# Where the rows of a gate come from: 32 matmuls in the first two expert passes, or a store and two broadcast loads

## The chip, the core and the metric

One NeuronCore of a Trainium2 chip runs the whole kernel. The metric is the device time in microseconds of one execution. TensorE (PE in the profile) multiplies matrices into eight PSUM banks, VectorE (DVE), ScalarE (ACT) and GpSimd (POOL) work element by element, SyncE (SP) does nothing but issue transfers, and 16 DMA engines carry them. ACT and POOL can issue transfers too.

## The reference, cut to what matters

One layer over 384 tokens of width 1024: 128 context tokens and 256 latent tokens. A modulation vector of six parts is computed from a conditioning vector, one vector for context tokens and one for latent tokens. After four token mixers comes a mixture of experts, and its output is scaled by the last of the six parts, `g2`, before it is added:

```
x = x + g1 * mix
h = _rmsnorm(x, p["norm2_g"]) * (1.0 + sc2) + sh2
x = x + g2 * _moe(h, p)
```

There are 64 experts; each token goes to eight. An expert has two matrices of 1024x256 (gate and up) and one of 256x1024 (down), so 3 MB of float32. After the last addition a final RMS norm is taken. `g2` differs between context and latent tokens but not between the tokens of one kind: tokens lie on partitions, so each of the two vectors is wanted as a row of 1024 repeated on all 128 partitions.

## The kernel before

The program has two parts. The *trunk* (projections, mixers, shared expert, router) runs to about 846 us of the span. Then `experts` (L2714) works on passes. A pass takes two experts of one slot `a_` (0 or 1): it gathers tokens (`xg`), multiplies by gate and up (job `H`), lets ACT and DVE form the hidden values, transposes them (`HT`), multiplies by down (`Y`) and scatters the result into PSUM banks 0 to 5 (`scatter`), where the sums of all tokens stay until the end. A round is two passes, slots 0 and 1. `body(0, "first")` is the first round, a hardware loop runs the others ("mid"; up to some count with four parts of a pass in 3+1, then in halves), and `body(n2, "last")` is one more pass.

Weights are double buffered by slot. SP issues them in `sync_part`: `refill` loads the four gate/up matrices of a slot (L3333, 1 MB each) once `H` of that slot is filled, and the two down matrices (L3337) once `Y` is filled. SP works its list in order. Ahead of the first refill it stores three tiles of token rows (L3347; the third waits for a GpSimd addition that itself waits for VectorE to have taken job `X 2`), then loads the final gain as a broadcast row (L3350), then waits for `X 2` and reads expert numbers out of SBUF.

The first round has extra jobs, since the assignment of experts to passes is still being planned: `X 0` to `X 4` are small matmuls of the plan (VectorE works between them), `G0` gathers, `S0` turns a selection, and `B 0` to `B 3` make the rows of the last gate. `gate_row` (L2874) is one `B` job: for each of four blocks of 128 channels two matmuls (a high and a low part) of a broadcast column of `mod_parts` with the identity, 8 matmuls into one PSUM bank, which ACT copies into `g2row` (L3022). All of these use banks 6 and 7, by the table `FIRST_BANKS`; a job waits until the job that had its bank before was read. `BETWEEN` says after which step `k` of `H` a job is put: `B 0` behind step 5 of the first `H`, `B 2` and `B 3` behind steps 4 and 6 of the second; `B 1` stands between the first `H` and `HT`. `mod_parts` is made by two VectorE operations (L2353, L2354) late in the trunk, and TensorE waits for them at L1181.

`g2row` is read only at the very end (L3257, L3260), when the expert sums are complete.

The first gate's rows go another way already: ACT stores `mod[:, 16:24]` to a DRAM tensor, one element per partition and channel block (L1681), and later loads it back as two broadcasts (L1701).

## Time and profile before

| | us |
|---|---|
| median of three runs | 1392.11 |
| lowest and highest of them | 1391.52, 1392.51 |
| span of the profiled execution | 1392.6 |
| PE busy | 1355.8 (97%) |
| DVE, ACT, POOL busy | 600.6, 390.8, 313.7 |
| granted TensorE clock | 9 or more tenths in 39 of 40 slices |
| DMA share by slice, from slice 25 of 40 | 9 tenths or more up to the last slice |

The span is the time from the first to the last instruction of one execution on the chip; the device times of the three other executions lie within 1.1 us of it. The profile gives for each engine how long it was busy; since matmuls are pipelined, a busy PE is not a PE at its peak. Times below are counted from the start of the span.

### The profile page before, as it was taken

Reading aid. Unit: us, or ns where it says so; the run is one execution under the profiler, and the core shown is the slowest. Engines: PE = TensorE matmul, PEld = TensorE weight load, DVE = VectorE, ACT = ScalarE, POOL = GpSimd, SP = SyncE. Lnnn points to the kernel's source line nnn. Section 1 sums busy time; section 2 is a strip of 40 time slices with the busy share of each in tenths; the row PEclk is TensorE's granted clock in tenths of the full one; section 3 lists DMA queues with packets and bytes.
Section 4 is the critical chain, followed back from the end, with each engine's and each line's share of the span. In section 5 each row is a group of like instructions: output and inputs, shape, how many; then the busy total and the mean of one; then the engine's idle time right before and its main releaser. Section 6 shows DMA issues by size and latency. Waiting matters only on the chain.

```text
span 1392.6 us, 20702 instructions
## 1 busy us (share of the span) xinstructions
PE 1355.8 (97%) x7716; PEld 950.3 (68%) x7716; DVE 600.6 (43%) x1347; ACT 390.8 (28%) x769; POOL 313.7 (23%) x248
## 2 busy tenths in 40 slices
PE   7999999999999999999999999999999999999996
PEld 2695898989988996788988875444445444444453
DVE  3467451885545486533322266333222332322224
ACT  3232221322544255233431141222112211221122
POOL 0431232243135553553333001101000000000001
PEclk9999999999999999999999999999999999999998
DMA  9640423133213336812144536999999999999992
GB/s 355 212 136 1 137 91 121 35 118 92 92 61 92 106 122 270 285 51 48 61 136 137 165 121 264 392 414 421 419 420 421 421 421 420 421 419 420 420 417 85
DMA packets 109744, 321.54 MB, mean 231 GB/s; under 512 B 12489, under 2 KB 72649, under 8 KB 81136
## 3 DMA queue, kind: packets, MB, share of 16 engines
q1 hardware_dynamic: 98416, 307.64, 57.6%
q0 software_dynamic: 2560, 8.81, 1.6%
q10 hardware_dynamic: 8704, 4.20, 1.1%
q8 instruction: 44, 0.72, 0.2%
q14 instruction: 20, 0.16, 0.0%
HBM read 320.08 MB, written 4.33 MB: 233 GB/s over the span
## 4 chain that ended last, share of the span: by engine, by line
PE 86%; DMA 9%; DVE 2%; ACT 1%; POOL 1%; issue 1%; SPq 0%; DVEq 0%; POOLq 0%
PE banks L650 21%; PE banks L617 20%; PE banks L2933 12%; DMA w<-in_exp_w 7%; PE banks L2980 7%; PE banks L2835 6%; PE banks L1057 3%; PE banks L2820 2%; PE banks L624 2%; PE banks L1201 1%; DMA ring<-in_ada_w 1%; PE banks L2828 1%; PE banks L769 1%; PE banks L889 1%; PE banks L701 1%; PE banks L1260 1%
## 5 line engine op out<-in xcount | busy, mean ns | idle before, releaser
L2933 PE MATMUL banks<-w,xg 128*64 128x512 f32 (+1 forms) x1312 | 235.8, 594 | 2.0 <-DMA w<-in_exp_w 1.9
L2933 PEld LDWEIGHTS banks<-w,xg 128*64 128x64 f32 (+1 forms) x1312 | 72.1, 126 | 150.9 <-issue 126.4
L650 PE MATMUL banks<-hT,ring 128*128 128x192 f32 x792 | 137.7, 327 | 0.2 <-DMA ring<-in_w_in 0.2
L3310 POOL DMA_INDIRECT fetched<-token_rows,row_of_place x32 | 32.1, 1004 | 443.2 <-DVE row_of_place L3111 433.1
L650 PEld LDWEIGHTS banks<-hT,ring 128*128 128x128 f32 x792 | 129.6, 190 | 2.1 <-DMA ring<-in_w_in 0.8
L2980 PE MATMUL banks<-w,hidT 128*64 128x512 f32 (+1 forms) x656 | 122.6, 600 | 0.3 <-DMA w<-in_exp_w 0.2
L2835 PE MATMUL banks<-y,selT 128*128 128x512 f32 x384 | 115.0, 415 | 0.0
L650 PE MATMUL banks<-x,ring 128*128 128x192 f32 x528 | 97.0, 327 | 0.9 <-ACT late L1377 0.9
L650 PE MATMUL banks<-x,combos 128*128 128x192 f32 x528 | 96.6, 326 | 0.0
L3122 DVE SCALAR_TENSOR_TENSOR hid<-banks,gslot,sil 128x256 f32<-128x256 f32 x33 | 16.0, 484 | 178.3 <-ACT sil L3015 177.7
L2835 PEld LDWEIGHTS banks<-y,selT 128*128 128x128 f32 x384 | 66.3, 189 | 35.1 <-issue 26.2
L650 PEld LDWEIGHTS banks<-x,ring 128*128 128x128 f32 x528 | 86.9, 190 | 1.4 <-ACT late L1377 1.2
L650 PEld LDWEIGHTS banks<-x,combos 128*128 128x128 f32 x528 | 87.6, 190 | 0.0
L617 PE MATMUL banks<-yT,ring 128*128 128x384 f32 x256 | 86.3, 487 | 0.9 <-ACT yT L1285 0.9
L617 PE MATMUL banks<-ring,hT 128*128 128x256 f32 x384 | 84.0, 379 | 0.0
L1285 ACT ACTIVATE arena<-banks 128x512 f32<-128x512 f32 (+2 forms) x91 | 49.7, 575 | 114.7 <-PE banks L617 57.1
L617 PEld LDWEIGHTS banks<-ring,hT 128*128 128x128 f32 x384 | 72.6, 190 | 10.2 <-issue 0.6
L2980 PEld LDWEIGHTS banks<-w,hidT 128*64 128x64 f32 (+1 forms) x656 | 32.1, 125 | 66.5 <-issue 46.8
L2480 POOL TENSOR_TENSOR ring<-ring,combos 128x512 f32<-128x512 f32 x33 | 44.9, 1360 | 131.4 <-PE banks L650 131.1
L3131 DVE TENSOR_TENSOR y<-banks,y 128x512 fp32r<-128x512 f32 x66 | 45.6, 691 | 62.5 <-ACT y L3034 62.5
L3015 ACT ACTIVATE sil<-banks 128x256 f32<-128x256 f32 x33 | 12.7, 384 | 201.4 <-PE banks L2933 201.4
L617 PEld LDWEIGHTS banks<-yT,ring 128*128 128x128 f32 x256 | 47.5, 190 | 29.3 <-issue 1.1
(482 smaller groups left out, 2033.4 us busy)
## 6 DMA issues: line engine op xcount, KB each, us to landing
w<-in_exp_w SPq DMA_DIRECT2D x198, 1024.0 KB, 13.9
ring<-in_w_in SPq DMA_DIRECT2D x46, 1024.0 KB, 5.5
ring<-in_ada_w SPq DMA_DIRECT2D x24, 1024.0 KB, 6.9
ring<-in_w_branch SPq DMA_DIRECT2D x8, 1024.0 KB, 6.6
ring<-in_w_out SPq DMA_DIRECT2D x4, 1024.0 KB, 6.6
arena<-in_sh_w SPq DMA_DIRECT2D x3, 1024.0 KB, 8.4
x<-in_x_sample SPq DMA_DIRECT2D x4, 512.0 KB, 8.3
token_rows<-whole_rows SPq DMA_DIRECT2D x3, 384.0 KB, 20.1
```

What stands on the lines that cost most here:

```text
L617: last = mm(out, lhsT=lhsT, rhs=rhs, start=i == 0, stop=i == len(pairs) - 1)
L624: last = nc.tensor.transpose(ps[0:n, i * P:(i + 1) * P], src, ident[:, :])
L650: last = mm(out, lhsT=w[:, k, :], rhs=tokens[:, k, :], start=start and k == 0, stop=k == KD // 2 - 1, skip_group_check=not start)
L1057: last = mm(ps[:, h * P:(h + 1) * P], lhsT=lhsT, rhs=rhs, start=True, stop=True)
L1285: banks.free(on(out, banks.at(act, key) if "src" not in kw else kw.pop("src"), func, **kw), key)
L2480: s_combos.on(g.tensor_tensor(a11, a12, combos[:, 1], ALU.subtract))
L2820: last = mm(out[:, i * 256:i * 256 + 256], lhsT=h2[part][:, t, k * P:(k + 1) * P], rhs=sel[:, t, :, :], start=n == 0, stop=n == 2 * NT - 1)
L2835: ins = mm(psum[:, t * 2 + h, :], lhsT=selT[:, a_, t * P:(t + 1) * P], rhs=y[:, part, h * W:(h + 1) * W], start=False, stop=False)
L2933: ins = mm(ps[lo:hi, :], lhsT=xg[:, k, a_ * P + lo:a_ * P + hi], rhs=w13[:, a_, u, :, k, :], start=k == 0, stop=k == KD - 1)
L2980: ins = mm(ps[lo:hi, :], lhsT=hidT[:, f, lo:hi], rhs=w2[:, a_, u, f, h * W:(h + 1) * W], start=f == 0, stop=f == 1)
L3131: ins = tt(y[:, LO, hh], ps, y[:, HI, hh].bitcast(F32), ALU.subtract)
L3310: nc.gpsimd.indirect_dma_start(fetched[:, a_, :], None, rows[:, :], bass.IndirectOffsetOnAxis(ap=row_of_place[:, 2 * a_:2 * a_ + 1], axis= ...
```

## The change

The rows of the last gate are no longer made by matmuls. ACT stores `mod[:, 40:48]` to a second DRAM tensor beside the first gate's, and SP loads it back as two broadcasts of 512 KB, behind the final gain and ahead of the first refill. The matmuls, the four jobs, the ACT copies, the two VectorE operations and the wait on them go; `X` jobs that had their bank after a `B` job now have it after another. VectorE waits for the two loads ahead of its first use of `g2row`.

```diff
-        mod_parts = sb("mod_parts", P, 2, KD, 2, dt=F32R)
+        sb("unused_parts", P, 4 * KD)
...
-            pe.wait_ge(s_row_parts.sem, 1)
...
                         act.dma_start(gate_rows[cnd].rearrange("(k p) -> p k", p=P), mod[:, 16:24, cnd],
                                       allow_slow_non_contiguous=True).then_inc(s_stored_gates.sem, 16)
+                        act.dma_start(last_gate_rows[cnd].rearrange("(k p) -> p k", p=P), mod[:, 40:48, cnd],
+                                      allow_slow_non_contiguous=True).then_inc(s_stored_last.sem, 16)
...
-            lane.link(v.tensor_copy(mod_parts[:, 0], mod[:, 40:48, :]))
-            s_row_parts.on(tt(mod_parts[:, 1], mod[:, 40:48, :], mod_parts[:, 0].bitcast(F32), ALU.subtract))
...
-                   ("X", 0, 1): 6, ("S0", 1, 0): 6, ("B", 0, 0): 6, ("X", 0, 2): 6, ("H", 0, 0): 7, ("B", 0, 1): 6, ("HT", 0, 0): 7,
-                   ("X", 0, 3): 6, ("Y", 0, 0): 7, ("X", 0, 4): 6, ("Y", 0, 1): 7, ("S", 0, 0): 7, ("S", 1, 0): 7, ("B", 0, 2): 7,
-                   ("B", 0, 3): 7}
+                   ("X", 0, 1): 6, ("S0", 1, 0): 6, ("X", 0, 2): 6, ("H", 0, 0): 7, ("HT", 0, 0): 7,
+                   ("X", 0, 3): 6, ("Y", 0, 0): 7, ("X", 0, 4): 6, ("Y", 0, 1): 7, ("S", 0, 0): 7, ("S", 1, 0): 7}
...
-               (0, 5): ("B", 0, 0), (0, 6): ("X", 0, 2), (1, 1): TURNS[0], (1, 2): TURNS[1], (1, 4): ("B", 0, 2), (1, 6): ("B", 0, 3)}
+               (0, 6): ("X", 0, 2), (1, 1): TURNS[0], (1, 2): TURNS[1]}
...
-                else:
-                    add_job(("B", 0, 1))
...
+        dve.wait_ge(s_g2, 32)
         for t in range(NT):
             dve.wait_ge(s_summed, t + 1)
             tt(gated[:, t, 0:W], psum[:, t * 2, :], g2row[:, min(t, 1), 0:W], ALU.mult).then_inc(s_gated, 1)
...
         sp.dma_start(fg_row[:, :], a["final_g"].rearrange("(a n) -> a n", a=1).to_broadcast([P, D])).then_inc(s_fg, 16)
+        sp.wait_ge(s_filled, 1)
+        sp.wait_ge(s_stored_last.sem, 32)
+        for cnd in range(2):
+            sp.dma_start(g2row[:, cnd, :], last_gate_rows[cnd].rearrange("(a n) -> a n", a=1).to_broadcast([P, D])).then_inc(s_g2, 16)
         sp.wait_ge(s_read["dve"], read(0, "dve", ("X", 0, 2), "first"))
```

## Rows read from the trace of the kernel before

**Rows 1.** Chain that ended last, in time order: start us, length us, what.

```profile
928.71 6.87 PE banks L2933 x64
...
1174.89 6.87 PE banks L2933 x32
...
1206.13 20.34 DMA w<-in_exp_w
...
1324.51 21.48 DMA w<-in_exp_w
```

**Rows 2.** Windows: stretch, length, busy us of five engines, PE clock, DMA share, GB/s.

```profile
875.00:1346.00 471.00, 468.40 (x2722) 223.28 (x2721) 139.86 (x387) 93.84 (x184) 31.12 (x31) 1.00 1.01 420
```

**Rows 3.** Tile of the expert weights: three slot-0 gate/up refills, issue and landing.

```profile
L3333 SPq DMA_DIRECT2D w<-in_exp_w x4: 333/354/1018, 919.4 to 920.9; - x4
DMA to landing us min/median/max: 8.5/11.5/14.7
...
L3333 SPq DMA_DIRECT2D w<-in_exp_w x4: 333/356/381, 1042.5 to 1043.9; - x4
DMA to landing us min/median/max: 10.6/13.6/17.1
...
L3333 SPq DMA_DIRECT2D w<-in_exp_w x4: 333/356/380, 1196.3 to 1197.8; - x4
DMA to landing us min/median/max: 12.5/15.9/21.6
```

**Rows 4.** Timeline, 865 to 884: start us, us, engine, line, operation, idle before.

```profile
865.81 0.34 PE L2868 MATMUL banks<-plan,late 64*1 64x24 f32 x4 [0.31 <-DVE plan L3194]
...
869.65 0.31 PEld L2949 LDWEIGHTS banks<-ident,hid 128*128 128x128 f32 x2 [0.21 <-DVE hid L3122]
...
870.27 0.17 PEld L2868 LDWEIGHTS banks<-plan,late 64*1 64x1 f32 x4 [0.30 <-ACT g2row L3022]
...
882.77 1.11 PE L2881 MATMUL banks<-ident_r,mod_parts 128*128 128x128 f32 x8
883.81 1.94 PE L2933 MATMUL banks<-w,xg 128*64 128x512 f32 x8
```

**Rows 5.** Timeline of GpSimd and of SP's queue, 868 to 905.

```profile
868.57 1.81 POOL L3299 TENSOR_TENSOR whole_rows<-h_high,h_low 128x768 f32<-128x768 f32 x1 [27.23 <-DVE quarter_gates L3202]
...
870.82 0.38 SPq L3350 DMA_DIRECT2D final_gain<-in_final_g  x1
...
873.11 2.02 SPq L3333 DMA_DIRECT2D w<-in_exp_w  x4
...
905.05 2.04 SPq L3333 DMA_DIRECT2D w<-in_exp_w  x4
```

**Rows 6.** Windows (as rows 2) where transfers ran below full rate.

```profile
719.90:723.90 4.00, 4.00 (x19) 3.07 (x19) 1.11 (x2) 0.70 (x2) 2.08 (x3) 1.00 0.84 276
722.00:723.00 1.00, 1.00 (x8) 1.00 (x7) 0.56 (x1) 0.00 (x0) 0.19 (x1) 1.00 0.94 377
871.10:875.00 3.90, 3.90 (x22) 2.12 (x21) 1.29 (x5) 0.60 (x1) 0.59 (x1) 1.00 0.98 269
905.00:908.00 3.00, 3.00 (x16) 2.54 (x16) 0.81 (x3) 1.13 (x3) 0.00 (x0) 1.00 0.98 388
937.00:939.00 2.00, 2.00 (x13) 1.70 (x12) 0.33 (x2) 0.83 (x2) 0.00 (x0) 1.00 0.97 360
```

**Rows 7.** Timeline round the first gate's store, 625 to 683.

```profile
625.94 1.01 ACTq L1681 DMA_DIRECT2D gate_rows<-mod  x2
629.86 0.33 ACT L1387 ACTIVATE late<-banks 128x192 f32<-128x192 f32 x1 [3.60 <-PE banks L650]
...
675.95 7.07 PE L617 MATMUL banks<-ring,hT 128*128 128x256 f32 x32
```

**Rows 8.** Tile of the ring: one slab's load and its landing.

```profile
L2599 SPq DMA_DIRECT2D ring<-in_w_in x1: 582/582/582, 621.1 to 621.1; - x1
...
DMA to landing us min/median/max: 14.6/14.6/14.6
```

More of the change, by code:

```diff
@@ L223, in trunk @@
         ident_r = sb("ident_r", P, P, dt=F32R)
-        mod_parts = sb("mod_parts", P, 2, KD, 2, dt=F32R)
-        gate_rows = nc.dram_tensor("gate_rows", (2, D), F32, kind="Internal").ap()
+        sb("unused_parts", P, 4 * KD)
+        gate_rows, last_gate_rows = (nc.dram_tensor(name, (2, D), F32, kind="Internal").ap()
+                                     for name in ("gate_rows", "last_gate_rows"))
         branches = ctx.enter_context(ExitStack())
@@ L470, in trunk @@
         s_madd = sig("branch_terms_added")
-        s_row_parts = sig("gate_row_parts_ready")
+        s_stored_last = sig("last_gate_rows_stored")
         s_stored_gates, s_g1 = sig("first_gate_rows_stored"), sig("first_gate_rows_landed")
@@ L603, in trunk @@
         s_w13 = [ctx.enter_context(nc.semaphore(f"gate_up_{a_}_landed")) for a_ in range(2)]
-        expert_work = experts(ctx, nc, a, o, psum, x, h2, mod_parts, ident_r, ident, ss, sq, sums, places, gates, iota, tiles, s_w13,
-                              s_rowsT.sem, s_out)
+        expert_work = experts(ctx, nc, a, o, psum, x, h2, last_gate_rows, ident_r, ident, ss, sq, sums, places, gates, iota, tiles, s_w13,
+                              s_rowsT.sem, s_out, s_stored_last)
         block = ctx.enter_context(nc.Block())
@@ L2711, in expert_tiles, with experts @@
     ])
-def experts(ctx, nc, a, o, psum, x, h2, mod_parts, ident_r, ident, ss, sq, sums, places, gates, iota, tiles, s_w13, s_rowsT, s_out):
+def experts(ctx, nc, a, o, psum, x, h2, last_gate_rows, ident_r, ident, ss, sq, sums, places, gates, iota, tiles, s_w13, s_rowsT, s_out, s_stored_last):
     def sem(name):
@@ L2753, in experts @@
     s_gated, s_added = sem("sums_gated"), sem("first_halves_added")
-    s_fg = sem("final_gain_landed")
+    s_fg, s_g2 = sem("final_gain_landed"), sem("last_gate_rows_landed")
     s_x = sem("second_halves_added")
@@ L2778, in readers @@
         kind, _, i = job
-        return {"H": ("act", "dve"), "HT": ("act",), "S": ("act",), "S0": ("act",), "Y": ("act", "dve"), "X": ("dve",), "B": ("act",),
+        return {"H": ("act", "dve"), "HT": ("act",), "S": ("act",), "S0": ("act",), "Y": ("act", "dve"), "X": ("dve",),
                 "G": (("act",), ("dve",))[i % 2], "G0": (("act",), ("dve",))[i % 2]}[kind]
@@ L2873, in plan_step @@
             return mm(out[:, NX:2 * NX], lhsT=rowsE[0:NE, 1, t * P:(t + 1) * P], rhs=one_hot, start=True, stop=True)
-        def gate_row(i, out):
-            cnd, h = divmod(i, 2)
-            for j in range(4):
-                for part in (HI, LO):
-                    c = mod_parts[:, part, h * 4 + j, cnd:cnd + 1]
-                    ins = mm(out[:, j * P:(j + 1) * P], lhsT=c.to_broadcast([P, P]), rhs=ident_r[:, :],
-                             start=part == HI, stop=part == LO)
-            return ins
         def body(q, kind, quarters):
@@ L2905, in add_job @@
                     close_bank(plan_step(i, open_bank(job)))
-                elif what == "B":
-                    close_bank(gate_row(i, open_bank(job)))
                 elif what == "G0":
@@ L3019, in take @@
                 ins = on(xg[:, 2 * i:2 * i + 2, :].rearrange("p k n -> p (k n)"), ps, ACT.Copy)
-            elif what == "B":
-                cnd, h = divmod(i, 2)
-                ins = on(g2row[:, cnd, h * W:(h + 1) * W], ps, ACT.Copy)
             elif what == "S0":
```

## The prediction

> **What bounds the kernel now.** The page comes first: PE is busy 97% of the span, which suggests that matmuls removed are time gained. It is an average over two different parts. From slice 25 on the line of DMA shares stands at 9 tenths or more, so the second view is the windows of that part: from 875 to 1346 us the engines moved 420 GB/s with a share of 1.01 and never rested [rows 2]. Two resources are near their limits at once, and the question is which one ends last.
>
> The chain of waits answers it round by round. Up to about 1206 us it runs through PE alone; rounds begin at 928.71 and, eight rounds later, at 1174.89, so PE needs (1174.89 - 928.71) / 8 = 30.8 us for one [rows 1]. Then the chain goes through transfers of expert weights of some 20 us each, the last of them issued at 1324.51 and waited for until 1346.0 [rows 1]. What follows 1346 is PE's fixed tail.
>
> How it comes to that is in the landings [rows 3]. The last of the four gate/up loads of slot 0 lands at 920.9 + 14.7 = 935.6, four rounds later at 1043.9 + 17.1 = 1061.0, five later at 1197.8 + 21.6 = 1219.4, and four later at 1346.0 [rows 1]. That is 31.35, 31.7 and 31.65 us a round, against PE's 30.8. The transfers are the slower stream from the start. They begin with a lead (a landing 14.7 us after its issue, where PE first has to wait at 21.6), lose 0.5 to 0.9 us of it a round, and at 1219 it is gone. So the end is set by one thing: when the stream of expert weights starts, and how much it must carry. A start x us later makes the kernel x us longer, and PE has 21.6 - 14.7 = 6.9 us of slack in the early rounds, to be used up by whatever PE saves there.
>
> **Part by part.**
>
> *The matmuls.* Each of the four jobs takes 883.81 - 882.77 = 1.04 us of PE [rows 4]: 4.2 us in all. On PE's own path the first one gives nothing: the plan job after it waits for VectorE anyway until 865.81 [rows 4], and with the bank job gone PE would only wait there longer. The second stood in the time in which `HT` waits for the hidden values, until 869.65 [rows 4]; it gives at most the 0.30 us by which the following plan job waited for ACT's copy of its bank [rows 4]. The last two give 2 x 1.04. PE is then 0.3 + 2.1 = 2.4 us earlier at the end of the first round. This is time that the slack of 6.9 us takes up: PE comes to wait for transfers some rounds sooner. On the path that ends last I count it as 0; its bounds are 0 and -2.4 us, the latter if the stream followed PE. The ACT copies and two small vector operations are beside PE's work: 0.
>
> *When the stream starts.* SP's first refill is issued at 873.11 [rows 5]. Ahead of it are VectorE's reading of `X 2`, GpSimd's addition at 868.57 of 1.81 us, the third store, the load of the final gain at 870.82, and 1.9 us in which SP reads the expert numbers [rows 5]. `X 2` starts when the plan is ready, at 865.8 as before, so nothing in this row moves forward. SP gets two more issues of 0.38 us: the refill is issued 0.8 us later. The two added waits are for things long past (the first bank filled in the first round, and a store of the trunk), so they hold up nothing that is queued behind them on SP, the refills.
>
> *What the stream carries.* The two broadcasts write 2 x 0.524 = 1.05 MB, and they are ahead of the refill in the same queue. At the stream's 420 GB/s that is 2.5 us [rows 2]. The nearest rows are the first gate's own two broadcasts: from 719.9 on they ran at 276 GB/s, 1.05 / 0.276 = 3.8 us; the first half of it is slow, while the window 722 to 723 has 377 GB/s, at which both would take 2.8 us [rows 6]. I take 2.8, because the new pair follows a broadcast that is already flowing (the final gain) as the second of that pair did, and keep 2.5 and 3.8 as ends. Now the shift. Between 871.1 and 875 the engines moved 269 GB/s x 3.9 us = 1.05 MB [rows 6], of which the third store and the final gain are 0.39 + 0.52 = 0.92; the remaining 0.13 MB are experts, worth 0.3 us at full rate. So the stream started as if at 875 - 0.3 = 874.7, and some 0.3 us earlier the gain was through. The new start is 874.4 + 2.8 = 877.2: 2.5 us later. Ends: 2.2 and 3.5. The 0.8 us of issue lie within it, since the queue is busy with the broadcasts meanwhile.
>
> *What comes back.* In the rounds where the lead in the queue was thinnest the rate dipped: 388 GB/s for 3 us from 905, just when SP issued a refill at 905.05, and 360 for 2 us from 937 [rows 5, 6]. Short of 420 that is 0.10 and 0.12 MB, 0.5 us together. With the stream later and PE's issues earlier, the queue is no longer near dry there. Up to 0.5 us may come back, or nothing if the engine that lands last was not the one that rested; I take 0.3.
>
> *The store.* Two issues more on ACT's queue, 1.0 us. ACT idled 3.60 us before its next operation at 629.86 [rows 7], so this is hidden; without that cover it would be 1.0 us at most. The transfers are 2048 elements of four bytes. Beside the ones that exist, a slab load issued at 621.1 took 14.6 us to land [rows 8], and twice as many elements may at most double that: 621.1 + 29.2 = 650.3. The slab belongs to the projection that PE starts at 675.95 [rows 7]: 25 us of cover, cost 0. The other slab of the time is issued ahead of it in the same queue and so landed earlier; if it too were held, GpSimd's work on it would be late, which I bound at +1 us, the length of the two added issues. The Trainium skill ("DMA: Bandwidth & Descriptors", Rules for kernel authors) says that a last dimension that isn't contiguous becomes one descriptor per element and is to be rearranged. [...]
>
> *The end.* VectorE's new wait ahead of `g2row` is for loads that land at about 878, 500 us before it: 0.
>
> Sum: 0 (matmuls) + 2.5 (stream later) - 0.3 (dips) + 0 (store) = +2.2 us. Against the profiled execution that is a span of 1392.6 + 2.2 = 1394.8; the median of the runs is 0.5 lower, 1392.1, so 1394.3 us.
>
> **Rivals.**
>
> *A. PE's time counts.* If the stream were paced by PE in the first rounds (the dips at 905 and 937 speak for it a little), the refills would come 2.4 us sooner. Against it: the rate is 420 GB/s nearly everywhere, and the landings come farther and farther apart from PE's round. 1392.1 - 2.4 = 1389.7; all four jobs at full price, 1387.9.
>
> *B. The loads are hidden.* A load asked for before the third store would have the engines to itself; SP, though, is held by that store until GpSimd's addition ends at 868.57 + 1.81 = 870.4 [rows 5], and these loads come behind it. For B it would need that broadcasts and weights overlap without sharing a rate: then only the 0.8 us of issue stays, less 0.3: 1392.6. The Trainium skill ("DMA: Bandwidth & Descriptors", Rules for kernel authors) advises to issue a DMA early and wait on its semaphore late, so that its setup overlaps with work; by it this change costs nothing, B's time. What the rule leaves out is that rows 2 show no free share of the engines.
>
> *C. A deeper queue is a slower queue.* Landings are 31.35 us apart in the first four rounds, 31.65 once the queue is deep [rows 3]. If depth itself is what costs (engines falling out of step, gathers behind more weights), then the new kernel, whose lead is gone from about the third round instead of the tenth, pays the 0.3 us difference in four or more rounds, +1.3 us, and no dip comes back: 1392.1 + 2.5 + 1.3 = 1395.9. It decides as soon as PE waits for weights before about 1100 us. Against it: both stretches show the same 420 GB/s.
>
> **How the numbers follow.** My forecast 0.50, with its own range 1393.3 to 1395.4; A 0.13; B 0.17; C, or the broadcasts at their slow end, 0.20. The time is that of the first, 1394.3. The range of 8 in 10 takes in the others in part: 1390.4 to 1396.6. A change of under 0.2% (2.8 us) is about what can't be told from none: below 1389.3 lies only the far half of A, 0.07; above 1394.9 lie C and a quarter of the forecast, 0.33; the rest, 0.60, is within.
>
> **What would show it.** Right: the refill issued near 873.9; the window 871 to 878 full of broadcasts; `X 2` on PE still at 865.8; slot 1's first refill issued some 2.4 us earlier than before; PE's first wait for expert weights well before 1206; the last such wait ending near 1348.2 instead of 1346.0, with the same 1392.6 - 1346.0 = 46.6 us behind it. Wrong: first refill's stream beginning before 876 (B), the last wait ending before 1346 (A), landings more than 31.6 us apart in the first rounds (C), or PE late anywhere before 860 (the store).

## The result: 1406.98 us, 1.0% slower

| | before | after |
|---|---|---|
| median, same chip | 1392.11 us (5 runs, 1391.52 to 1395.13) | 1406.98 us (5 runs, 1404.59 to 1409.39) |
| span of the profiled execution | 1392.6 us | 1407.2 us |
| ratio, 95% interval | | 1.010, 1.0088 to 1.0112 |

The forecast was 1394.3 us with a range up to 1396.6. The change is slower by 14.9 us in the medians and by 14.6 us in the two profiled spans, and the loss is in three places, two of which (the store and the removed matmuls) the prediction had costed at nothing. One execution of all runs below, of the kernel with the turned rows, had a mean TensorE clock of 0.946 and took 1426.65 us; it is left out.

**The page after.** TensorE is busy 0.9 us longer, although 32 matmuls are gone. ACT's queue (q10) has 10,784 packets in place of 8,704, and they take 2.1% of the DMA engines' time in place of 1.1%: of the 2,080 packets more, 2,048 are the new store's elements of four bytes, 8 KB together.

```profile
PE 1356.7 (96%) x7684; PEld 947.1 (67%) x7684; DVE 599.6 (43%) x1345; ACT 388.0 (28%) x765; POOL 313.8 (22%) x248
q10 hardware_dynamic: 10784, 4.21, 2.1%
```

**The end of the loop.** First the chain of waits after, the answer to [rows 1] (start us, length us, what). It goes through the expert weights from 1157 us on instead of from 1206, and the last landing is at 1338.62 + 21.71 = 1360.3 where it was 1346.0: 14.3 us late. What follows it is 46.9 us against 46.6. So the whole loss is there when the loop ends.

```profile
1157.19 20.01 DMA w<-in_exp_w
...
1338.62 21.71 DMA w<-in_exp_w
```

Next the timelines of two engines after, first TensorE's with two of its waits, then SP's queue from 868 to 920 us; the answer to [rows 4, 5]. The final gain is issued at 878.37 instead of 870.82, so 7.55 us of the 14.3 are there before any expert weight is reloaded. The refill follows 2.99 us behind it (before: 2.29), the down matrices are issued at 888.33, and by 917.62 the list is 12.57 us behind the 905.05 of [rows 5].

```profile
872.92 0.34 PE L2867 MATMUL banks<-plan,late 64*1 64x24 f32 x4 [1.50 <-DVE plan L3176]
...
903.09 1.09 PE L2827 MATMUL banks<-ident,fetched 128*128 128x128 f32 x8 [2.06 <-DMA fetched<-token_rows,row_of_place]
...
878.37 0.38 SPq L3333 DMA_DIRECT2D final_gain<-in_final_g  x1
878.85 0.92 SPq L3337 DMA_DIRECT2D g2row<-last_gate_rows  x2
881.36 2.35 SPq L3316 DMA_DIRECT2D w<-in_exp_w  x4
888.33 0.81 SPq L3320 DMA_DIRECT2D w<-in_exp_w  x2
...
917.62 2.12 SPq L3316 DMA_DIRECT2D w<-in_exp_w  x4
```

**The trunk: 7.55 us between these two traces, 10.3 from the store on.** The change does nothing before the first gate's store, and that store is issued at 625.94 before [rows 7] and at 623.19 after. So the execution traced after was 2.75 us ahead when the change began to act. That is a difference between two executions and no gain: the two windows below, first before and then after, show one place where they differ: the granted clock is 0.86 in the trace before and 1.00 in the one after. The columns are stretch, length, busy us with counts for PE, PEld, DVE, ACT, POOL, PE clock, DMA share, GB/s. From the store to the final gain it is 870.82 - 625.94 = 244.9 us before and 878.37 - 623.19 = 255.2 us after, 10.3 us more. The ledger of the 14.3 us is -2.75 + 10.3 in the trunk and 6.75 in the expert part.

```profile
388.00:400.00 12.00, 11.60 (x84) 11.16 (x83) 5.96 (x22) 9.65 (x21) 0.00 (x0) 0.86 0.53 175
388.00:400.00 12.00, 11.60 (x97) 11.11 (x97) 7.28 (x24) 11.23 (x29) 1.14 (x1) 1.00 0.53 176
```

Where the 10.3 us go: windows after, 630 to 650 us. While the DMA engines are busy and move almost nothing (share 2.01, 5 GB/s), TensorE works 1.89 of 5 us and then 0 of 5, and its granted clock goes to half (0.69 and 0.62 are means over windows in which it changed).

```profile
630.00:635.00 5.00, 5.00 (x31) 3.94 (x31) 0.24 (x1) 3.07 (x6) 3.50 (x3) 1.00 1.59 1
635.00:640.00 5.00, 1.89 (x17) 1.69 (x15) 0.56 (x1) 0.00 (x0) 1.00 (x1) 1.00 2.01 5
640.00:645.00 5.00, 0.00 (x0) 0.00 (x0) 0.00 (x0) 0.41 (x1) 0.00 (x0) 0.69 0.83 25
645.00:650.00 5.00, 4.71 (x18) 3.91 (x19) 2.32 (x6) 1.33 (x3) 1.27 (x1) 0.62 0.77 167
```

The timeline of the same stretch shows who stood still (start us, us, engine, line, operation, idle before). ACT issues the four stores from 623.19 on, one of them in 2.85 us; that is the cover of 3.6 us of [rows 7], now 4.25, and harmless. Then at 636.9 TensorE's block of matmuls L1058 ends in the records, ACT should copy its bank, and no engine does anything until 644.59: ACT rests 10.52 us, VectorE 9.52, TensorE 8.40, GpSimd 11.39.

```profile
623.19 0.37 ACTq L1681 DMA_DIRECT2D gate_rows<-mod  x1
623.60 0.60 ACTq L1683 DMA_DIRECT2D last_gate_rows<-mod  x1
624.23 2.85 ACTq L1681 DMA_DIRECT2D gate_rows<-mod  x1
...
634.94 1.95 PE L1058 MATMUL banks<-arena 128*128 128x128 f32 x16
...
644.59 0.60 ACT L1285 ACTIVATE arena<-banks 128x512 f32<-128x512 f32 x1 [10.52 <-remote]
645.22 0.69 DVE L2345 TENSOR_TENSOR arena<-arena 128x512 f32<-128x512 f32 x1 [9.52 <-ACT arena L1285]
...
645.29 1.09 PE L625 MATMUL banks<-ident,arena 128*128 128x128 f32 x4 [8.40 <-issue]
...
648.16 1.27 POOL L2574 TENSOR_TENSOR arena<-arena,levels 128x512 f32<-128x512 f32 x1 [11.39 <-PE banks L1058]
```

What ACT waited for is called "remote" in this view, but the trace's records of semaphores, which none of the views prints, have it: it is TensorE's own count of filled banks. It rises at 644.57 and 644.66, which is 8.6 and 7.8 us after the recorded ends (635.99 and 636.88) of the two matmuls that raise it; before, it rises 0.02 us after each of the same two. GpSimd's count rose meanwhile, at 636.78, 0.01 us after its addition ended. So TensorE's signals were late, and not all signals; the other engines stood behind them. No load of program code is in the trace between 626 and 649 us, so the rest is no wait for one.

**The other 6.75 us (14.3 - 7.55), in the expert part.** Windows after. From 878.6 to 886 the engines moved 276 GB/s x 7.4 us = 2.04 MB, of which third store, gain and broadcasts are 1.97; the 0.07 MB of experts are 0.2 us at full rate, so their stream starts as if at 885.8, where it was 874.7: 11.1 us late, or 3.55 more than the trunk. Between 917 and 920 the queue runs dry at 191 GB/s, (419 - 191) x 3 / 419 = 1.6 us.

That leaves 1.6 us. Most of it is no late stream but a wider spread inside a group of four loads. The last two lines are the landings of the last four gate/up loads, before and after: the first lands at 1323.1 + 11.0 = 1334.1 and 1337.2 + 9.4 = 1346.6, 12.5 us late, the last 14.3 us late. The stream as a whole is thus some 12.7 us late (7.55 + 3.55 + 1.6), and TensorE waits for the last load of the four. What spreads them isn't shown.

```profile
878.60:886.00 7.40, 7.40 (x28) 3.91 (x28) 1.82 (x7) 0.98 (x2) 0.64 (x1) 0.62 0.95 276
872.00:882.00 10.00, 7.92 (x28) 4.30 (x30) 4.49 (x21) 0.77 (x2) 3.12 (x2) 0.60 0.31 94
910.00:917.00 7.00, 7.00 (x66) 1.98 (x64) 2.06 (x5) 0.60 (x1) 0.00 (x0) 1.00 1.01 410
917.00:920.00 3.00, 3.00 (x18) 2.32 (x15) 0.48 (x1) 1.11 (x3) 0.00 (x0) 1.00 0.64 191
920.00:1360.00 440.00, 436.86 (x2528) 206.97 (x2526) 130.03 (x360) 86.70 (x171) 28.93 (x29) 1.00 1.01 419
...
L3333 SPq DMA_DIRECT2D w<-in_exp_w x4: 333/357/381, 1323.1 to 1324.5; - x4
DMA to landing us min/median/max: 11.0/14.7/21.5
...
L3316 SPq DMA_DIRECT2D w<-in_exp_w x4: 333/356/381, 1337.2 to 1338.6; - x4
DMA to landing us min/median/max: 9.4/13.5/21.7
```

In this execution the granted clock was 0.60 in the window from 872 to 882, behind the 1.50 us in which TensorE waited for VectorE's plan with the first gate-row job gone ([rows 4]: 0.31). 0.50 is the 1.2 GHz level, 1.00 the 2.4 GHz level.

### The profile page after: what moved, and what is told of

Same layout as the page of the kernel before. It is cut to its first block, busy times and chain, and to the rows that moved or that the text cites. A ratio compares the mean times of both kernels' runs of the same rounds, so it can differ in the third digit from the quotient of the medians.

```text
span 1407.2 us, 20637 instructions
## 1 busy us (share of the span) xinstructions
PE 1356.7 (96%) x7684; PEld 947.1 (67%) x7684; DVE 599.6 (43%) x1345; ACT 388.0 (28%) x765; POOL 313.8 (22%) x248
## 3 DMA queue, kind: packets, MB, share of 16 engines
q10 hardware_dynamic: 10784, 4.21, 2.1%
q0 software_dynamic: 2560, 8.81, 1.6%
## 4 chain that ended last, share of the span: by engine, by line
PE 81%; DMA 13%; DVE 2%; issue 2%; ACT 1%; POOL 1%; SPq 0%; POOLq 0%; DVEq 0%
PE banks L651 21%; PE banks L618 20%; PE banks L2920 11%; DMA w<-in_exp_w 10%; PE banks L2965 7%; PE banks L2834 5%; PE banks L1058 3%; PE banks L2819 2%; PE banks L625 2%; PE banks L1201 1%; DMA ring<-in_ada_w 1%; PE banks L2827 1%; PE banks L890 1%; PE banks L770 1%; PE banks L702 1%
## 5 line engine op out<-in xcount | busy, mean ns | idle before, releaser
L2965 PE MATMUL banks<-w,hidT 128*64 128x512 f32 (+1 forms) x656 | 125.7, 610 | 0.5 <-DMA w<-in_exp_w 0.3
L3000 ACT ACTIVATE sil<-banks 128x256 f32<-128x256 f32 x33 | 12.7, 384 | 209.7 <-PE banks L2920 209.7
```

What stands on the lines that cost most here:

```text
L2965: ins = mm(ps[lo:hi, :], lhsT=hidT[:, f, lo:hi], rhs=w2[:, a_, u, f, h * W:(h + 1) * W], start=f == 0, stop=f == 1)
```

## Experiments: the change taken apart

Each time below is the median of 4 to 12 executions, with the lowest and the highest. "Before" is the kernel before on the same chip and at the same time: 1392.62 us for the first four, 1393.07 for the next four, then 1392.99, 1391.94 and 1392.44.

**The change without its store.** The broadcasts read the first gate's rows, so the output is not the reference's.

```diff
-        expert_work = experts(ctx, nc, a, o, psum, x, h2, last_gate_rows, ident_r, ident, ss, sq, sums, places, gates, iota, tiles, s_w13,
-                              s_rowsT.sem, s_out, s_stored_last)
+        expert_work = experts(ctx, nc, a, o, psum, x, h2, gate_rows, ident_r, ident, ss, sq, sums, places, gates, iota, tiles, s_w13,
+                              s_rowsT.sem, s_out, s_stored_gates)
...
-                        act.dma_start(last_gate_rows[cnd].rearrange("(k p) -> p k", p=P), mod[:, 40:48, cnd],
-                                      allow_slow_non_contiguous=True).then_inc(s_stored_last.sem, 16)
```

> The changed kernel without the added store of elements; the two broadcasts read the first gate's rows instead, so the last gate's values are not the reference's. Theory S (the store's 2048 four-byte packets hold up the trunk: in the changed kernel every engine rests for 8.4 us at 637 to 645): the rest goes, the trunk ends 7.4 us earlier, about 1399.6 us. Rival (the rest comes from something else that was changed, such as the removed wait or the two vector operations): still about 1407.

Measured: 1398.14 us (1396.0 to 1399.16), ratio 1.0038 (1.0024 to 1.0052). The store carries some two thirds of the loss.

**The removal alone.** No store and no loads; `g2row` is set to ones by GpSimd, so the last gate is left out.

```diff
-        for cnd in range(2):
-            sp.dma_start(g2row[:, cnd, :], last_gate_rows[cnd].rearrange("(a n) -> a n", a=1).to_broadcast([P, D])).then_inc(s_g2, 16)
...
+        nc.gpsimd.memset(g2row[:, :, :], 1.0).then_inc(s_g2, 1)
```

> The matmuls, their jobs and copies are removed and nothing is put in their place: no store, no loads; the rows of the last gate are set to 1 by GpSimd, so that gate is left out of the result. Theory C (the hole left by the first job makes TensorE rest, its clock falls to half for 10 us, the later passes are late and the transfer queue runs dry): slower than before by 3 to 5 us, 1395 to 1397, with half clock near 867 to 877 and a dip in transfers near 910. Rival L (only the loads cost anything): 1392 or a little below.

Measured: 1394.39 us (1392.46 to 1400.04), ratio 1.0015 (1.0004 to 1.0026). Taking 32 matmuls out of a kernel whose TensorE is busy 97% of the time makes it slower, not faster, though by less than the 3 to 5 us that I had expected. In its windows TensorE runs at half clock behind the hole, and by 902 to 912 the weights are below full rate:

```profile
864.00:874.00 10.00, 8.84 (x26) 3.38 (x24) 3.30 (x14) 0.77 (x2) 4.86 (x3) 0.51 0.56 179
...
902.00:912.00 10.00, 10.00 (x80) 4.84 (x76) 3.69 (x12) 2.94 (x6) 2.00 (x2) 1.00 0.97 375
```

**The two broadcasts alone**, in the kernel before: they load the first gate's rows into `g2row`, and the `B` jobs stay, but ACT copies their banks (192 columns) into a scratch tile.

```diff
-                ins = on(g2row[:, cnd, h * W:(h + 1) * W], ps, ACT.Copy)
+                ins = on(tiles["scratch"][:, :], ps[:, 0:192], ACT.Copy)
...
+            sp.dma_start(g2row[:, cnd, :], gate_rows[cnd].rearrange("(a n) -> a n", a=1).to_broadcast([P, D])).then_inc(s_g2, 16)
```

> The kernel before with only the two broadcast loads added (of the first gate's rows); the matmul jobs stay and their copies go to a scratch, 192 columns each, so the last gate's values are not the reference's. If the stream's later start passes through to the end: +3.5 us, 1395.6 (broadcasts at some 280 GB/s). If broadcasts run at the stream's rate: +2.2, 1394.3. Theory C says no half clock here. Rival (hidden): 1392.5.

Measured: 1396.18 us (1394.61 to 1398.13), ratio 1.0022 (1.0013 to 1.0031). In the chain of this kernel (as above) TensorE waits for weights from 1082 us on. The last landing is at 1327.70 + 21.46 = 1349.2 instead of 1346.0, with the final gain issued at 870.56 instead of 870.82: 3.5 us for the pair, as expected. Behind the chain stand windows of this kernel. By 878 the engines had moved 259 GB/s x 3.8 + 300 x 3.4 us = 2.00 MB, of which 1.97 are third store, gain and broadcasts, so the weights start as if at 877.9, 3.2 us later than before. The last two are the places of the dips of [rows 6], and the dips are gone (before: 388 and 360 GB/s).

```profile
1082.63 20.41 DMA w<-in_exp_w
...
1327.70 21.46 DMA w<-in_exp_w
...
870.80:874.60 3.80, 3.80 (x22) 2.01 (x20) 1.33 (x5) 0.60 (x1) 0.63 (x1) 1.00 0.88 259
874.60:878.00 3.40, 3.40 (x18) 1.06 (x16) 2.73 (x9) 0.60 (x1) 0.00 (x0) 1.00 0.74 300
905.00:908.00 3.00, 3.00 (x19) 2.58 (x17) 0.81 (x4) 0.83 (x2) 0.00 (x0) 1.00 1.02 423
937.00:939.00 2.00, 2.00 (x16) 1.65 (x19) 0.55 (x4) 0.83 (x2) 0.00 (x0) 1.00 1.03 430
```

**The store alone**, added to the kernel before; nothing reads it.

```diff
+                        act.dma_start(last_gate_rows[cnd].rearrange("(k p) -> p k", p=P), mod[:, 40:48, cnd],
+                                      allow_slow_non_contiguous=True).then_inc(s_stored_last.sem, 16)
```

> The kernel before with only the second store of elements added beside the first gate's. Theory S: +7.4 us, 1399.5, with the same rest of all engines after 637. Rival (the store is hidden and the rest needs the other edits): 1392.

Measured: 1402.3 us (1400.28 to 1404.58), ratio 1.0069 (1.0055 to 1.0083). The same rest stands in its trace, TensorE idle 8.61 us until 645.68, and from the first gate's store to the final gain it is 255.4 us, 10.5 more than before. The parts add up, each as its median over 1392.62: store 9.7, loads 3.6, removal 1.8, together 15.0 (unrounded), against 14.9 for the whole. Loads and removal together are 5.3, and the run without the store had 5.5.

## Experiments: what it is about the store

**Half of it**: the kernel before with the second store for one condition only.

```diff
+                        if cnd: act.dma_start(last_gate_rows[cnd].rearrange("(k p) -> p k", p=P), mod[:, 40:48, cnd],
+                                      allow_slow_non_contiguous=True).then_inc(s_stored_last.sem, 16)
```

> The kernel before with the second store for one condition only: 1,024 elements more than before, where the full second store has 2,048 and cost 9.6 us (1402.3 against 1392.6). Theory 1, the loss grows with the number of single-element packets in flight: in proportion it gives +4.8 us, 1397.4 us, and the rest of all engines near 637 to 644 us is shorter. Theory 2, there is a number of packets below which nothing happens (the 2,048 of before show no rest): 1392.5 to 1394 us. Theory 3, the number of issued stores counts and not the packets: near three quarters or more of the full loss, 1399 us or above.

Measured: 1393.88 us (1391.99 to 1395.49), ratio 1.0001 (0.9992 to 1.0010). Not in proportion: 1,024 packets more cost at most 1.4 us, 2,048 cost 9.7. The trace still has a small rest of the same kind: TensorE 2.26 us until 646.93, and again the semaphore records show TensorE's own counts rising 3.0 and 1.8 us after the ends of their matmuls. From the first gate's store to the final gain this execution takes 247.4 us, 2.5 more than before; it is the slowest of the eleven (1395.49 us). So a hold is first seen with the 3,072 elements of the three stores, and little of it reaches the median. Packets of ACT's queue between 620 and 660 us take 3.8% of the engines' time before (2,080 packets), 9.3% here (3,120) and 37.7% after (4,160): 11.7 ns, 19 ns and 58 ns recorded for one packet (share x 16 engines x 40 us / packets). Recorded packets overlap where the share is above 1, as in the windows above, so the last is no time that an engine gave to one packet alone.

```profile
646.45 0.33 ACT L1372 ACTIVATE gate<-banks 128x192 f32<-128x192 f32 x1 [3.75 <-remote]
...
646.93 1.54 PE L652 MATMUL banks<-x,combos 128*128 128x192 f32 x8 [2.26 <-ACT gate L1372]
```

**The same numbers in 64-byte pieces.**

```diff
+                    act.dma_start(packed_rows, mod[:, 40:48, :].rearrange("p k c -> p (k c)")).then_inc(s_stored_last.sem, 16)
```

> The kernel before with one added store of the same 2,048 numbers at the same place, but as 64 contiguous bytes of each partition (nothing reads it). If the single-element packets are what holds the engines, this costs 0 to +1 us (1392.4 to 1393.6 us) and ACT's issue is short. If any transfer that ScalarE adds there costs the time, it comes out near the 1402.3 us of the store by elements.

Measured: 1393.37 us (1391.5 to 1395.45), ratio 1.0000 (0.9991 to 1.0009). The cost is the packets, not the transfer or its issue. That one issue takes 3.28 us, longer than the 2.85 us above (I had expected a short one), so a long issue is not the loss here either. The Trainium skill ("DMA: Bandwidth & Descriptors", Rules for kernel authors) says that a last dimension that isn't contiguous becomes one descriptor per element and should be rearranged; this pair of runs prices the rule here, 9.7 us against nothing.

**The store moved to 713 us**, the end of ACT's part of the delta mixer, in the changed kernel.

```diff
             fill("end")
+            for cnd in range(2):
+                act.dma_start(last_gate_rows[cnd].rearrange("(k p) -> p k", p=P), mod[:, 40:48, cnd],
+                              allow_slow_non_contiguous=True).then_inc(s_stored_last.sem, 16)
             act.wait_ge(s_stored_gates.sem, 16 * 2)
```

> The changed kernel with its added store issued at the end of the delta stage (near 715 us) in place of at 623 us. Theory: the loss of the store is that of its place, inside the levels of the inverse, where every engine hands over to the next each microsecond; at 715 us ScalarE has few hand-overs ahead, so the time falls to that of the kernel without the store, 1398 us (1397 to 1400). Rival: the packets hold the engines wherever they are issued, so 1405 to 1409 us, with a rest of all engines behind 715 us in the trace.

Measured: 1407.14 us (1405.54 to 1412.72), ratio 1.0106 (1.0089 to 1.0124). My theory fell: nothing was won. But the rival's picture is not what the trace shows either. Its timeline has a plain reason: ACT's next four issues stand behind the element packets in the same queue and take 4.45 and 9.34 us (before: 0.82 and 1.25), so ACT rests 14.31 us ahead of its next operation (before: 1.55), and TensorE waits 8.81 us for it.

```profile
713.53 1.00 ACTq L1700 DMA_DIRECT2D last_gate_rows<-mod  x2
714.57 4.45 ACTq L1704 DMA_DIRECT2D arena<-gate_rows  x2
719.07 9.34 ACTq L1708 DMA_DIRECT2D out_new_gdn<-arena  x2
728.43 1.28 ACT L1394 ACT_TABLE_LOAD   x1 [14.31 <-issue]
...
731.03 2.90 PE L651 MATMUL banks<-x,combos 128*128 128x192 f32 x8 [8.81 <-ACT gate L1370]
```

**The store moved to 655 us**, away from both neighbours.

```diff
+                    if (r, l) == (2, 4):
+                        for cnd in range(2):
+                            act.dma_start(last_gate_rows[cnd].rearrange("(k p) -> p k", p=P), mod[:, 40:48, cnd],
+                                          allow_slow_non_contiguous=True).then_inc(s_stored_last.sem, 16)
                     s_gmix.on(on(in_blocks(gmix, m), both_ways(GXT + r * 2 * W, m), ACT.Copy))
```

> The changed kernel with its added store issued at the fourth level of the last inverse, near 660 us: some 36 us behind the store of the first gate's rows and 55 us ahead of ScalarE's next transfers. Theory 1, what costs is how many single-element packets are in flight together, or what ScalarE issues behind them: each store alone drains in some 15 us, so the engines never rest for 8 us and the time is that of the change without its store, 1398 us, ratio 1.003 to 1.005. Theory 2, it is the total of 4,096 packets, or a second such store anywhere: 1405 to 1407 us, ratio 1.009 to 1.011.

Measured: 1402.08 us (1401.14 to 1405.34), ratio 1.0075 (1.0062 to 1.0088): between the two theories, 0.0037 or 5.2 us above the run without the store, 3.5 and 4.3 us below the same kernel with the store early and late (1.0100 and 1.0106). Nobody stands still now, and ACT's issues take 1.0 us. The victim is a third one: SP's ring load of 661.62 takes 10.5 us to land (before: 5.4), and TensorE waits for it 3.93 us and then runs at 0.64 clock for 4.8 us.

```profile
672.21 2.75 PE L651 MATMUL banks<-hT,ring 128*128 128x192 f32 x8 [3.93 <-DMA ring<-in_w_in]
...
672.20:677.00 4.80, 4.79 (x19) 4.79 (x20) 0.00 (x0) 0.54 (x2) 4.47 (x4) 0.64 0.32 120
```

So one store has three ways to cost, by its place: TensorE's signals come late and all engines stand behind them, the issuer's next transfer stands behind it, another queue's load lands late. Each way is read from one or two traces. The Trainium skill ("DMA: Bandwidth & Descriptors", Queues, rings and completion order) has it that each DMA engine takes turns between the queues it has work for, packet by packet; the late ring load agrees with it (10.5 us instead of 5.4).

## Experiments: the loads and the hole

**The broadcasts behind the last refill**, in the kernel without the store.

```diff
             refill(q, 0, bass.ds(2 * q, 1), "mid")
+
...
+        for cnd in range(2):
+            sp.dma_start(g2row[:, cnd, :], gate_rows[cnd].rearrange("(a n) -> a n", a=1).to_broadcast([P, D])).then_inc(s_g2, 16)
```

> The changed kernel without its added store, its two broadcast loads (of the first gate's rows) moved from ahead of the first refill to behind the last one. Theory 1, the pair costs 3.6 us because it stands ahead of the weight stream: moved, the time is that of the removal alone, 1394.4 us, ratio 1.001 to 1.002, and in the trace the pair lands by 1360 us, before its first use near 1377 us. Rival: the loads cost the same wherever they stand (they share the engines with the last landings, or the end waits for them): ratio 1.0035 to 1.004 as before the move.

Measured: 1393.63 us (1392.5 to 1400.2), ratio 1.0011 (1.0000 to 1.0022); ahead of the refill it was 1.0038, and the removal alone had 1.0015. The pair is issued at 1346.6, lands later than expected, by 1347.0 + 20.7 = 1367.7, and is first used at 1377.0. The 3.6 us are the price of the place, and all of it comes back.

```profile
L3238 DVE TENSOR_TENSOR w<-banks,g2row x3: 680/680/682, 1377.0 to 1378.2; 128x512 f32<-128x512 f32 x3
...
L3353 SPq DMA_DIRECT2D g2row<-gate_rows x2: 335/380/424, 1346.6 to 1347.0; - x2
...
DMA to landing us min/median/max: 14.4/17.6/20.7
```

**The final gain behind the last refill too**, in the kernel before, with the plan's wait and the reading of the expert numbers put ahead of the third store: the same lever pulled the other way.

```diff
             e = [sp.value_load(expert_of[0:1, u, at], min_val=0, max_val=NE - 1) for u in range(2)]
+            if kind == "first":
+                whole(NT - 1)
...
             refill(q, 0, bass.ds(2 * q, 1), "mid")
+
...
+        sp.dma_start(fg_row[:, :], a["final_g"].rearrange("(a n) -> a n", a=1).to_broadcast([P, D])).then_inc(s_fg, 16)
```

> The kernel before with only SyncE's list changed: the wait for the plan and the reading of the experts' numbers stand ahead of the third rows store, and the broadcast load of the final gain stands behind the last refill in place of ahead of the first. Theory 1, all that stands ahead of the weight stream is paid in full: the first refill is issued 2 to 3 us earlier and the stream is one load of the final gain (some 1.5 us) shorter, so 3 to 4 us faster, 1389 to 1390 us, ratio 0.997 to 0.998. Rival: TensorE, not the stream, sets the end over much of the loop, so the stream's start gives back 1 us or nothing: ratio 0.999 to 1.000.

Measured: 1393.2 us (1391.81 to 1395.4), ratio 0.9999 (0.9990 to 1.0008). A miss. The first refill is issued at 871.00 instead of 873.11, but the next are issued at 888.05 and 905.12, where they were at 887.98 and 905.05, because they wait for TensorE to empty a slot. The queue runs out of work meanwhile and the 2.1 us are lost again. In the windows of this kernel:

```profile
890.00:895.00 5.00, 4.65 (x32) 3.55 (x32) 1.32 (x3) 1.28 (x3) 0.00 (x0) 1.00 0.95 364
905.00:910.00 5.00, 5.00 (x32) 3.51 (x36) 1.98 (x8) 1.29 (x4) 1.00 (x1) 1.00 0.92 316
```

The same windows before had 414 and 398 GB/s. So the stream's start is a bound in one direction only here: later (the pair) costs in full, 2.1 us earlier gives nothing.

**Fillers in the holes**: the removal alone, with eight matmuls of the identity by itself in the place of the first removed job, then also in that of the second. A third has the first filler on the kernel with the late store.

```diff
+                    for j in range(8):
+                        ins = mm(ps[:, j // 2 * P:(j // 2 + 1) * P], lhsT=ident_r[:, :], rhs=ident_r[:, :], start=j % 2 == 0, stop=j % 2 == 1)
```

> The run with the removal alone (no store, no loads, the gate rows set to one), with eight matmuls of an identity by itself in the place of the first removed gate-row job. Theory 1, the removal made the kernel slower (ratio 1.0015) because of the hole that it left before TensorE's plan job, behind which the granted clock fell to 0.50 for 10 us: filled, the mean clock is back at 0.996 to 0.997 and the time at or below that of before, ratio 0.998 to 1.000. Theory 2, the loss is in the other three removed jobs, or in a changed order of the banks: ratio 1.001 to 1.003 as without the filler.

> The run with the removal alone, with fillers of eight matmuls of an identity by itself in the places of the first two removed gate-row jobs (ahead of the plan job, and between the first pass's first product and its turn). Theory 1, the loss by the removal (ratio 1.0015, executions with a mean clock of 0.991 to 0.995) is the holes: with both filled every execution has a mean clock of 0.995 or more as the kernels with all gate-row jobs have, and the time is 1391 to 1393 us, ratio 0.9985 to 1.000. Theory 2, the holes of the second pass or other things are it: some executions stay at 0.994 or below and the ratio at 1.0005 to 1.0015.

> As the run with the late store, and in the place of the removed first gate-row job TensorE runs eight matmuls of an identity by itself into a scratch bank (a filler, of no use to the result). Theory: the hole of the removed job lets TensorE's granted clock fall to 0.50 in some executions and puts the first refills late; filled, the clock stays at 1.00 and the time is 1 to 2.5 us below that of the late store alone, near 1396.5 us. Rival: the hole costs nothing by itself and the filler adds its own 0.5 us: same time or 0.5 us above.

Measured: one filler 1393.86 us (1390.81 to 1398.89), ratio 1.0009 (0.9997 to 1.0022); two 1392.67 us (1391.3 to 1395.82), 1.0005 (0.9997 to 1.0014); with the late store 1407.2 us, 1.0098 (1.0084 to 1.0113), no different from the same kernel unfilled. By the times alone neither theory is settled: the intervals overlap that of the bare removal. The clocks say more. Executions with a mean granted clock of 0.994 or less: 10 of 11 with the bare removal, 6 of 12 with one filler, 3 of 12 with two, and 0 of the 113 executions of the kernel before that were taken beside the experiments. So holes do cost clock, and filling them brings it back in part; I had expected all of it. Within one kernel the clock and the time go together: with one filler the six executions at 0.993 or 0.994 took 1394.29 to 1398.89 us and the six at 0.996 or 0.997 took 1390.81 to 1393.43. It need not be the removal's whole price, though: the run without the store has the same matmuls removed and mean clocks of 0.995 to 0.996, and the parts still add up to its time. Where the rest is, the profiled execution with two fillers shows. With 2.1 us less work in the second pass TensorE comes early to the fetched rows (`fetch` is issued at 881.50, before: 881.52), and waits:

```profile
892.01 1.10 PE L2826 MATMUL banks<-ident,fetched 128*128 128x128 f32 x8 [2.03 <-DMA fetched<-token_rows,row_of_place]
...
892.00:896.00 4.00, 3.65 (x16) 2.11 (x18) 1.97 (x7) 0.60 (x1) 0.00 (x0) 0.62 1.00 416
```

The last two removed jobs are turned into a wait of 2.03 us and a second fall of the clock.

**The change mended**: store at 655 us, both fillers, broadcasts last.

> The whole change, mended in three places: the added store near 660 us, fillers in the places of the first two removed jobs, and the two broadcast loads behind the last refill. If the costs of the store, of the stream's late start and of the holes were all there was, nothing is left of the 14.4 us: 1391 to 1394 us, ratio 0.999 to 1.001, and no gain either, since the 16 matmuls that stay away are not on the path of the weight stream. If a cost remains that the theory does not know: above 1395 us.

Measured: 1398.21 us (1397.14 to 1401.52), ratio 1.0049 (1.0036 to 1.0061). Above my range. The theory left out that the store still costs at this place: 5.2 us there and 0.7 of the removal with two fillers make 5.9, against 6.3 for the whole.

**Without an added element store.** The first gate's stays. SyncE's list is in the order of the run with the final gain last. One gate-row job is left, of two matmuls that turn the 16 columns into 16 rows of 512 bytes; these are stored as they are and broadcast back behind the last refill.

```diff
+            for part in (HI, LO):
+                ins = mm(out[0:2 * KD, 0:P], lhsT=mod_parts[:, part].rearrange("p c k -> p (c k)"), rhs=ident_r[:, :],
+                         start=part == HI, stop=part == LO)
...
+        sp.dma_start(last_gate_rows.rearrange("c (k p) -> (c k) p", p=P), tiles["turned"][:, :]).then_inc(s_rows_out, 16)
```

> The order of SyncE's list as in the run with the final gain last, and the change made another way: of the four gate-row jobs (32 matmuls) one is left, of two matmuls that turn the last gate's 16 columns into 16 rows of 512 bytes; these are stored contiguously after the first refill, and the two broadcast loads stand behind the last refill. Theory: neither the held engines nor the stream's late start are there, so at least as fast as the run with the final gain last, 1388 to 1390 us, ratio 0.996 to 0.998. Rival: the hole of the removed matmuls (only two of eight stay in the first job) lowers the clock again and takes 1 to 2 us back: 1390 to 1392 us.

Measured: 1393.32 us (1390.12 to 1396.08), ratio 0.9996 (0.9983 to 1.0008), clocks 0.993 to 0.997. The 1388 to 1390 us of the theory did not come. The same with both holes filled:

> The run with the turned rows (ratio 0.9996, mean clocks of 0.993 to 0.997 and one outlier), with the first gate-row job filled up to eight matmuls and the second one's place filled by eight matmuls of an identity by itself. Theory, the holes are what scatters the clock: all executions at 0.995 or above, no outlier, and a ratio of 0.999 to 1.000, 1391 to 1393 us; nothing is gained over the kernel before, since the sixteen matmuls left out are beside the weight stream. Rival: the scatter stays as it was, so it comes from the second pass's removed jobs or from the loads at the end: clocks down to 0.993 again and a ratio of 0.9995 to 1.001.

Measured: 1391.53 us (1390.06 to 1396.06), ratio 0.9998 (0.9988 to 1.0008), as expected, but two of twelve clocks at 0.994. These two are the only forms of the change that are not slower, and neither is faster than the kernel before by anything that can be measured.

## Why the prediction was wrong, by its own steps

- **What bounds the kernel**: right as far as it went. The loop's end moved by what the stream lost, and the tail stayed (46.9 against 46.6 us). "A start x us later makes the kernel x us longer" held (3.5 to 3.6 us for the broadcasts). Its other direction, that an earlier start would gain, was never needed for the sum and is false (ratio 0.9999).
- **The matmuls, 0 (bounds 0 and -2.4)**: wrong in sign. The step said "with the bank job gone PE would only wait there longer". It waited 1.50 us instead of 0.31, as said, but a wait was not neutral: the granted clock fell to half behind it in the traces of the change and of the removal alone (mean clock 0.994 or less in 10 of the latter's 11 executions), and in the trace with two fillers the saved time of the second pass ended in a wait for fetched rows. Measured +1.8 us (ratio 1.0004 to 1.0026); a bound below 0 only was the mistake. How much of it the clock is stays open.
- **When the stream starts, +2.5 (ends 2.2 and 3.5)**: right mechanism, size off. The refill came 2.99 us behind the gain instead of 2.29, so the 0.8 us of issue were right; with the loads alone the weights started 3.2 us later, 3.5 with the final gain's own 0.26 us, and the pair cost 3.5 us at the loop's end, 3.6 in the medians. I had picked the rate of the second half of the older pair's transfer; the mean rate of that whole pair, 3.8 us [rows 6], was the nearer row.
- **What comes back, -0.3**: the mechanism came with the loads alone, where the dips were gone (423 and 430 GB/s), but the loop's end gained nothing by it: 3.5 us late at the start, 3.5 at the end. In the whole change the queue ran dry at 917 us instead, since the third refill was issued 12.57 us late, 5.0 more than the trunk, behind TensorE's half clock and its wait for fetched rows.
- **The store, 0 (up to +1)**: the failed step, 9.7 of the 14.9 us. It asked only when the slab beside it would land. That slab, now issued at 618.4, landed in 12.2 us, and the next one, issued at 629.8, in 22.8 instead of 9.9; no engine waited for either, so that part held. But twice the packets made TensorE's signals 8 us late and the engines rest 8.4 us and more, and no row of before showed such a thing at half the dose. The forecast's own sign for it, TensorE late before 860, is the one that came. The bound "+1, the length of the two added issues" bounded a different mechanism.
- **The end, 0**: right; the loads land 500 us before their use.
- **Rivals**: A and B are out. C's conditions came (TensorE waits for weights before 1100 us in the run with the loads alone), but not its extra cost of 1.3 us: landings of that run are 31.5 us apart in the first four rounds and the shift at the end is 3.5 us, the pair itself. What was missing is a rival in which the store holds up the trunk, at a price of its own: 9.7 us of the forecast's error of 12.7 lie there.

## What to carry to other kernels

A store that breaks into thousands of packets of a few bytes is to be costed by its neighbours at that place (who signals whom, what its issuer issues next, which load is in flight), and first of all avoided: here the same numbers in 64-byte pieces cost nothing. Work taken from beside the bound was worth nothing here and left a hole; two loads on the bounding queue cost 3.6 us ahead of its transfers and nothing behind the last one that somebody waits for. A bound of a step should also hold the case that the step is harmful, even where it only takes work away. And two traces are compared from the point where the change begins to act, not from their start: here that is the difference between 7.55 and 10.3 us.

## What the hardware did that I had not expected

- With 4,160 packets of ACT's queue between 620 and 660 us, all four compute engines rested 8.4 to 11.4 us; with 2,080 there was no such rest, with 3,120 one of 2.3 us, with 64-byte pieces none. The runs show that the packets are the cause. What was late is TensorE's count of filled banks, 8.6 us after the recorded end of its matmul (8.8 with the store alone, 3.0 with half of it), while GpSimd's count came in 0.01 us. Ends of matmuls are modelled, so whether the matmul itself, its writing or only its signal was held is not shown.
- The recorded time of one such packet grew with their number: 11.7, 19 and 58 ns.
- Four transfers issued behind them in the same queue took 4.45 and 9.34 us to issue, and ScalarE rested 14.3 us.
- TensorE's granted clock went to 0.50 behind an idle piece of 1.50 us, and not each time: in the trace of the run without the store the same piece of 1.50 us, until 865.19, left it at 1.00. What decides it is open.
